# First norm applied on leaving PSUM, its transposes inside the first two projection slots, masks by quarters

## The chip, the cores and the metric

The kernel runs on one core of a Trainium2 chip. The metric is its device time in microseconds (us). The engines are TensorE (PE, its weight loads PEld), VectorE (DVE), ScalarE (ACT), GpSimd (POOL) and SyncE (SP), which only issues transfers here. Each works through its own list of instructions in order and waits on semaphores.

## What is computed

A decoder trunk of two layers on 1024 tokens of width 1024, all in float32. The first layer's mixer is what the change touches:

```
def rmsnorm(x, g):
    xf = x.astype(jnp.float32)
    y = xf * lax.rsqrt(jnp.mean(xf * xf, axis=-1, keepdims=True) + EPS)
    return (y * g.astype(jnp.float32)).astype(x.dtype)
...
    h = rmsnorm(x, norm_mix[layer])
    if layer % 2 == 0:
        x = x + even_mixer(h, positions, ...)
    ...
    h = rmsnorm(x, norm_mlp[layer])
    x = x + sq_relu_mlp(h, mlp_w_up[layer], mlp_w_down[layer])
```

`even_mixer` projects h and splits the columns into 4 retention heads and 8 heads of dilated attention, whose queries and keys are normed and rotated. A query sees the keys at distances 0, 1, .. 128, at multiples of 4 up to 512 and at multiples of 16 up to 2048; a key seen by two or three patterns counts twice or three times. So the score of a distance gets a summand that depends on the distance alone: nothing, minus log 2 or log 3, or a large number that takes the key out (the scores are kept negated). Then follow the output projection, an MLP, and the second layer with windowed attention and an MLP.

## The kernel before

Tokens stand in T = 8 tiles of 128 partitions, X[:, i, :]. Every product is done in three passes over split operands: a matrix is kept as a rounded part (hi) and the rest (lo), and hi*hi + hi*lo + lo*hi is summed in PSUM. Weights come in by SyncE into `raw` in pieces of two blocks of 128 rows (128 x 768 for a projection). ScalarE writes W_hi (`split_hi`, L620), GpSimd writes W_lo (`split_lo`, L1209), and SyncE may load the next but one piece when W_lo of a piece is done (`w_ready`).

The start (phase DR) works like this. GpSimd fills a table of distances `di` (L1313) and small constants. VectorE's `masks` makes `nlm`, the summand by distance, for all 1024 distances in 14 instructions (L867 to L886). ScalarE makes 16 exponentials for the retention decay (L806 to L809). Then for each of the eight token tiles ScalarE squares and sums (`square`, L626), GpSimd takes the root (`norm_rstd`, L1214, L1216), VectorE multiplies by the token's factor and the gain (`normed`, L943), TensorE transposes eight blocks (L360) into `sc` or `tp` in turn, ScalarE copies the rounded part to hT_hi (L630) and VectorE writes hT_lo (`lo_T`, L933). Only then are the four pieces of the first projection split, and VectorE computes the angles (L891 to L918).

After that `dr_slots` runs 66 slots. Slot s projects one token tile (24 matmuls, 128x384 each, L350 to L352): slots 0 to 7 those of two heads of dilated attention, 8 to 15 those of one retention head, and so on for four groups. In slot t, ScalarE evacuates the product of slot t-1 into G (`evac_G`, L637) and squares it (L652); VectorE sums (L1006), GpSimd multiplies by the gains (L1225) and takes the roots (L1239, L1241), VectorE norms and rotates (`prep`, L1015 to L1027), TensorE transposes (`heads_T`, L441) and ScalarE copies these to qT and kT. Two units of attention go along, each in steps: `scores` (L400), `maxima` (L1044), `probs` (L672), `trans` (L422), `probs_T` (L664), `values` (L434), `outputs` (L1064, L1066). A new `values` waits until `outputs` of the unit before has read o_ps. In slots 2 to 5 of each eight a piece of the next weights is split as well.

What sets the order is the order in which each engine's function writes its instructions: there is no scheduler. Slot by slot and half by half (j = 0, 1), each engine's `dr_slots` lists its steps.

## Time and profile before

| | us |
|---|---|
| median of 3 runs | 2614.97 |
| lowest and highest | 2613.98, 2615.36 |
| the profiled execution | 2612.44 |
| its span | 2610.7 |
| TensorE busy in it | 2486.2 (95%) |
| VectorE, ScalarE, GpSimd busy | 1075.7, 739.6, 806.7 |

The page says how busy each engine is in 40 slices of 65 us; the chain of waits follows the last instruction back to the start; the timeline lists instructions with their start, duration and what ended the idle time before them. Times are from the start of the span. A matmul's duration reaches beyond the start of the next, so the distance of two starts tells the pace.

### The profile page before, as it was taken

The numbers are of one execution on the slowest core, as the hardware profiler recorded it, in microseconds if no ns is written. First come the engines' busy times: TensorE is split into PE (matmuls) and PEld (weight loads), VectorE is DVE, ScalarE is ACT, GpSimd is POOL, SyncE is SP. The second block draws the span as 40 slices with busy tenths as digits, with TensorE's granted clock in tenths as the row PEclk, the third lists the DMA queues.
The fourth block names the chain that finished last, engine by engine and source line by source line (L and its number), as shares of the span: only waits on it lengthen the run. The fifth ranks groups of instructions, "written<-read, shape, count | busy, mean of one in ns | idle before, by whom it ended". The sixth has DMA issues, their size and how long they took to land.

```text
span 2610.7 us, 34016 instructions
## 1 busy us (share of the span) xinstructions
PE 2486.2 (95%) x12520; PEld 2080.3 (80%) x12520; DVE 1075.7 (41%) x2591; ACT 739.6 (28%) x1487; POOL 806.7 (31%) x770
## 2 busy tenths in 40 slices
PE   5999999998989999999999799999989999999998
PEld 4787878787968888888887688879978888888886
DVE  7464645454323232323233566662322323232323
ACT  4424343331221212121221355552312121212220
POOL 4223132310333333333332233331133333333331
PEclk9999999998999999999999899998999999999999
DMA  3000000002211111111111200003011111111111
GB/s 115 25 25 25 25 25 25 25 19 80 69 33 49 48 48 48 48 48 48 48 48 43 89 26 25 25 25 103 31 49 49 48 48 48 48 48 48 48 48 65
DMA packets 108200, 120.20 MB, mean 46 GB/s; under 512 B 26048, under 2 KB 94144, under 8 KB 108096
## 3 DMA queue, kind: packets, MB, share of 16 engines
q1 hardware_dynamic: 100720, 103.70, 12.8%
q10 hardware_dynamic: 7376, 15.12, 1.7%
q8 instruction: 64, 1.05, 0.2%
q14 instruction: 40, 0.33, 0.0%
HBM read 110.41 MB, written 8.39 MB: 46 GB/s over the span
## 4 chain that ended last, share of the span: by engine, by line
PE 84%; DVE 8%; POOL 3%; ACT 2%; issue 2%; DMA 0%; POOLq 0%; SPq 0%; ACTq 0%; DVEq 0%
PE gp L350 11%; PE gp L352 10%; PE gp L351 10%; PE sc L350 5%; PE sc L352 4%; PE sc L351 4%; PE tp L351 4%; PE tp L352 4%; PE tp L350 4%; PE o_ps L434 4%; PE sc L400 3%; PE tp L422 2%; PE o_ps L350 2%; PE qt L350 2%; PE qt L351 2%; PE o_ps L352 2%
## 5 line engine op out<-in xcount | busy, mean ns | idle before, releaser
L1209 POOL TENSOR_TENSOR W_lo<-raw,W_hi 128x1024 fp32r<-128x1024 f32 (+2 forms) x200 | 433.7, 2183 | 704.1 <-ACT W_hi L620 704.0
L350 PE MATMUL gp<-W_hi,hT_hi 128*128 128x384 f32 (+1 forms) x1152 | 421.9, 366 | 14.8 <-POOL W_lo L1209 6.7
L352 PE MATMUL gp<-W_hi,hT_lo 128*128 128x384 f32 (+1 forms) x1152 | 384.3, 334 | 0.0
L351 PE MATMUL gp<-W_lo,hT_hi 128*128 128x384 f32 (+1 forms) x1152 | 383.9, 333 | 0.0
L620 ACT ACTIVATE W_hi<-raw 128x1024 fp32r<-128x1024 f32 (+2 forms) x200 | 186.4, 964 | 646.7 <-PE qt L352 559.0
L1148 DVE TENSOR_TENSOR r<-r 128x512 f32<-128x512 f32 x128 | 92.2, 720 | 626.8 <-ACT r L773 626.8
L1295 POOL TENSOR_TENSOR a_lo<-r,a_hi 128x512 fp32r<-128x512 f32 x128 | 166.0, 1298 | 447.5 <-ACT a_hi L775 447.5
L1155 DVE TENSOR_TENSOR X<-tp,X 128x512 f32<-128x512 f32 x256 | 176.8, 692 | 173.8 <-PE tp L352 171.7
L350 PEld LDWEIGHTS gp<-W_hi,hT_hi 128*128 128x128 f32 x1152 | 221.2, 192 | 26.9 <-issue 11.2
L351 PEld LDWEIGHTS gp<-W_lo,hT_hi 128*128 128x128 f32 x1152 | 221.6, 192 | 0.0
L352 PEld LDWEIGHTS gp<-W_hi,hT_lo 128*128 128x128 f32 x1152 | 219.9, 191 | 0.0
L350 PE MATMUL gp<-hT_hi,W_hi 128*128 128x512 f32 x512 | 201.5, 393 | 16.0 <-POOL W_lo L1209 16.0
L350 PE MATMUL tp<-W_hi,a_hi 128*128 128x512 f32 x512 | 204.1, 399 | 11.7 <-POOL W_lo L1209 11.7
L350 PE MATMUL sc<-hT_hi,W_hi 128*128 128x512 f32 x512 | 200.9, 392 | 5.3 <-DVE hT_lo L933 5.3
L351 PE MATMUL tp<-W_lo,a_hi 128*128 128x512 f32 x512 | 204.1, 399 | 0.0
L352 PE MATMUL tp<-W_hi,a_lo 128*128 128x512 f32 x512 | 203.9, 398 | 0.0
L352 PE MATMUL gp<-hT_hi,W_lo 128*128 128x512 f32 x512 | 200.4, 391 | 0.0
L352 PE MATMUL sc<-hT_hi,W_lo 128*128 128x512 f32 x512 | 200.4, 391 | 0.0
L351 PE MATMUL sc<-hT_lo,W_hi 128*128 128x512 f32 x512 | 200.2, 391 | 0.0
L351 PE MATMUL gp<-hT_lo,W_hi 128*128 128x512 f32 x512 | 200.1, 391 | 0.0
L434 PEld LDWEIGHTS o_ps<-V,pT 128*128 128x128 f32 x1056 | 138.5, 196 | 15.8 <-issue 8.7
L434 PE MATMUL o_ps<-V,pT 128*128 128x64 f32 x1056 | 136.8, 274 | 11.1 <-DVE X L1066 7.0
(187 smaller groups left out, 4083.8 us busy)
## 6 DMA issues: line engine op xcount, KB each, us to landing
raw<-in_mlp_w_up SPq DMA_DIRECT2D x64, 512.0 KB, 3.8
raw<-in_mlp_w_down SPq DMA_DIRECT2D x64, 512.0 KB, 3.2
raw<-in_hyb_w_in SPq DMA_DIRECT2D x80, 128.0 KB, 2.5
X<-in_x SPq DMA_DIRECT2D x8, 512.0 KB, 12.0
X<-in_x ACTq DMA_DIRECT2D x8, 512.0 KB, 3.2
raw<-in_swa_w_qkv SPq DMA_DIRECT2D x16, 256.0 KB, 2.7
x_spill<-X ACTq DMA_DIRECT2D x8, 512.0 KB, 2.6
X<-x_spill ACTq DMA_DIRECT2D x8, 512.0 KB, 3.3
```

The source lines that it names most:

```text
L350: mm(o, a[0], b[0], start=first, stop=False)
L351: mm(o, a[0], b[1], start=False, stop=False)
L352: return mm(o, a[1], b[0], start=False, stop=last)
L400: last = mm(sc[:, c:e], qT[r, a % 2, 0:P], kT[r, c:e], start=True, stop=True)
L422: last = nc.tensor.transpose(tp[:, to:to + P], Pm[:, j, c:c + P], ident[:, :])
L434: last = mm(o_ps[:, e * HD:(e + 1) * HD], pT[:, j, to:to + P], V[:, c, v0:v0 + HD], start=(m == 0 or bl[m - 1][3] != e), stop=(m == len(bl ...
L620: A(W_hi[:, slot, n * p:n * (p + 1)], raw[:, p % 2, 0:n], ACT.Copy).then_inc(w_hi, 1)
L1148: E.tensor_tensor(r2[:, ft, :], r2[:, ft, :], r2[:, ft, :], ALU.mult).then_inc(a_sq, 1)
L1155: E.tensor_tensor(x, d_out[(2 * i + nh) % D_BANKS], x, ALU.add).then_inc(d_evac, 1)
L1209: E.tensor_tensor(W_lo[:, slot, c], raw[:, p % 2, 0:n], W_hi[:, slot, c].bitcast(f32), ALU.subtract).then_inc(w_ready, 1)
L1295: E.tensor_tensor(a_lo[par][:, ft, r], r2[:, ft, :], a_hi[par][:, ft, r].bitcast(f32), ALU.subtract).then_inc(a_ready, 1)
```

## The change

The norm of the first layer's mixer is taken apart. The gain is multiplied in ahead of the transposes (`first_gain`, into a new buffer xn0), while the token's factor, a number per row of the product, is applied by ScalarE when it evacuates the projection (`evac_G`, now with a scale from `nscale`). Tiles 0 and 2 get their gain from VectorE, 1 and 3 to 7 from GpSimd. The transposes of tile 0 come ahead of the first slot, those of the others at places inside slots 0 and 1 (`FIRST_T`). The squares and roots of tiles 2 to 7 move to the ends of slots 1 to 6. The pieces of the first weights are loaded and split between the first token tiles. `masks` makes only the last 256 of 1024 columns of nlm, which the first units of attention read, and `far_masks` makes the other three quarters in slot 3, ahead of `outputs`. The exponentials (`powers`) move with the load of the retention gains from the start to the end of slot 7, and what VectorE does with them (`decays`) to the start of slot 8. W_hi and W_lo get other addresses, so that xn0, the gain g0 and the angles lie in halves of them that aren't used yet. In the diff, "..." marks what is left out.

```diff
-            sp.dma_start(gA[:, :], bcast(norm_mix[0], D)).then_inc(g_full, 16)
-            for i in range(1, T):
+            sp.dma_start(g0[:, :], bcast(norm_mix[0], D)).then_inc(g_full, 16)
+            load_D(0, P_DR, (0, 1))
+            for i in range(1, 4):
                 sp.dma_start(X[:, i, :], xt[:, i, :]).then_inc(x_full[i], 16)
-            load_D(0, P_DR)
+            load_D(0, P_DR, (2, 3))
+            for i in range(4, T):
+                sp.dma_start(X[:, i, :], xt[:, i, :]).then_inc(x_full[i], 16)
             load_R(0, P_DR + 4)
             for g in range(1, NG):
...
+            def first_T(s, q):
+
+                for i in range(T):
+                    if FIRST_T[i] == (s, q):
+                        norm_T(0, i, 0, 0)
+
+            FIRST_T = [(0, 0), (0, 2), (0, 4), (1, 1), (1, 2), (1, 3), (1, 4), (1, 4)]
...
+                        if s < 2 and j == 0:
+                            first_T(s, 0)
                         next(steps)
                         next(steps)
+                        if s < 2:
+                            first_T(s, 2 * j + 1)
...
-                A(G[:, (t - 1) % RING, :], gp[:, (t - 1) % 2, 0:W], ACT.Copy).then_inc(gemm_evac, 1)
+                i = (t - 1) % T
+                act.wait_ge(rstd_ready, i + 1)
+                A(G[:, (t - 1) % RING, :], gp[:, (t - 1) % 2, 0:W], ACT.Identity,
+                  scale=nscale[:, i:i + 1]).then_inc(gemm_evac, 1)
...
+            def powers():
+
+                act.wait_ge(ss_ready, T)
+                act.dma_start(gnB, bc(gn_gain[0].rearrange("h d -> (h d)"), RH * RV)).then_inc(const_in, 16)
+                for h in range(RH):
+                    A(decay[:, h, :], dq[:, 0:P], ACT.Exp, scale=LG[h])
+                    A(xi[:, h:h + 1], dq[:, P:P + 1], ACT.Exp, scale=LG[h])
+                    A(zeta[:, h:h + 1], dq[:, P + 1:P + 2], ACT.Exp, scale=LG[h])
+                    last = A(cdec[:, h:h + 1], dq[:, P + 2:P + 3], ACT.Exp, scale=LG[h])
+                step.did(last)
...
+                            if s == 1:
+                                for i in ((3, 4), (5, 6, 7))[j]:
+                                    copy_T(i, 0, 0)
                             if j == 1 and 0 <= t - 1 < T:
                                 heads_T_copy("D", t, a0)
+                        if j == 1 and 1 <= s < T - 1:
+                            square(0, s + 1)
+                        if j == 1 and s == T - 1:
+                            powers()
...
-            for i in range(T + 1):
-                if i < T:
-                    act.wait_ge(x_full[i], 16)
-                    square(0, i)
-                if i >= 1:
-                    copy_T(i - 1, 0, 0)
-            for p in range(4):
-                split_hi(p, 0, W, 16 * KQ * (p // 2 + 1))
+            for p in range(2):
+                split_hi(p, 0, W, 16 * KQ)
+                copy_T(p, 0, 0)
+                act.wait_ge(x_full[p], 16)
+                square(0, p)
+            for p in (2, 3):
+                split_hi(p, 0, W, 2 * 16 * KQ)
             act.wait_ge(dve_step, SETUP_SIN)
...
+            def mask_of(o, counts):
+                step.wait()
+                step.did(E.tensor_scalar(o, t2[:, :], 0.0, BIG, ALU.is_equal, ALU.mult))
...
+            def far_masks():
+
+                step.did(E.tensor_tensor(t2[:, :], m4[:, :], m16[:, :], ALU.add))
+                mask_of(nlm[:, 2 * MW:3 * MW], (2.0,))
+                step.wait()
+                step.did(E.scalar_tensor_tensor(t2[:, :], df[:, :], 512.0 - 2 * MW, m4[:, :], ALU.is_le, ALU.mult))
+                step.wait()
+                step.did(E.tensor_tensor(t2[:, :], t2[:, :], m16[:, :], ALU.add))
+                mask_of(nlm[:, MW:2 * MW], (2.0,))
+                step.did(E.tensor_scalar(nlm[:, 0:MW], m16[:, :], 0.0, BIG, ALU.is_equal, ALU.mult))
+                step.wait()
...
+            def decays():
+                dve.wait_ge(act_step, 2)
                 dve.wait_ge(const_in, 16 * 5)
...
+            def first_gain(i):
+                dve.wait_ge(g_full, 16)
+                dve.wait_ge(x_full[i], 16)
+                if i >= 2:
+                    dve.wait_ge(nt_done, i - 1)
+                E.tensor_tensor(xn0[:, i % 2, :], X[:, i, :], g0[:, :], ALU.mult).then_inc(xn_ready, 1)
...
+                    if s == T:
+                        decays()
                     for j in range(2):
+                        if s == 3 and j == 1:
+                            far_masks()
...
             masks()
-            for i in range(T + 1):
-                if i < T:
-                    normed(0, i, 0)
-                if i >= 1:
-                    lo_T(i - 1, 0, 0)
+            first_gain(0)
+            lo_T(0, 0, 0)
             angles()
+            lo_T(1, 0, 0)
+            first_gain(2)
+            lo_T(2, 0, 0)
...
+                        if s == 1:
+                            for i in (5, 6, 7):
+                                first_gain(i)
...
-                norm_rstd(0, i)
-            for p in range(4):
-                split_lo(P_DR, p, 0, 2 * W)
-            pool.wait_ge(const_in, 16 * 5)
+            split_lo(P_DR, 0, 0, 2 * W)
+            split_lo(P_DR, 1, 0, 2 * W)
+            first_gain(1)
+            norm_rstd(0, 0)
+            norm_rstd(0, 1)
+            split_lo(P_DR, 2, 0, 2 * W)
+            split_lo(P_DR, 3, 0, 2 * W)
+            first_gain(3)
+            first_gain(4)
+            pool.wait_ge(const_in, 16 * 4)
...
```

On TensorE, the end of the first transposes and the start of the first product, before (xnA is the normed tile, sc and tp the halves of PSUM that take transposes):

```order
L360 MATMUL sc<-ident,xnA 128x128 [waits ht_ready,xn_ready]
L360 MATMUL sc<-ident,xnA 128x128 x7
L360 MATMUL tp<-ident,xnA 128x128 [waits ht_ready,xn_ready]
L360 MATMUL tp<-ident,xnA 128x128 x7
L350 MATMUL gp<-W_hi,hT_hi 128x384 [waits w_ready,ht_ready,gemm_evac]
L351 MATMUL gp<-W_lo,hT_hi 128x384
L352 MATMUL gp<-W_hi,hT_lo 128x384
```

And after, in the middle of slot 0 (xn_75 is xn0):

```order
L365 MATMUL gp<-W_hi,hT_hi 128x384
L366 MATMUL gp<-W_lo,hT_hi 128x384
L367 MATMUL gp<-W_hi,hT_lo 128x384
L375 MATMUL tp<-ident,xn_75 128x128 [waits xn_ready]
L375 MATMUL tp<-ident,xn_75 128x128 x7
L365 MATMUL gp<-W_hi,hT_hi 128x384 [waits w_ready]
L366 MATMUL gp<-W_lo,hT_hi 128x384
L367 MATMUL gp<-W_hi,hT_lo 128x384
```

The transposes of tile 1 now stand between the fourth and fifth block of slot 0's product, and the product waits there for its weights.

On ScalarE, from the first evacuation (G<-gp) to the second and the first exponential of the attention, before:

```order
L637 ACTIVATE G<-gp 128x384 [waits gemm_done]
L652 ACTIVATE sq<-G 128x256 [waits gemm_evac]
L686 ACTIVATE qT<-qt 128x128 [waits qt_done]
L688 ACTIVATE kT<-qt 128x128
L637 ACTIVATE G<-gp 128x384 [waits gemm_done]
L652 ACTIVATE sq<-G 128x256 [waits h_ss,gemm_evac]
L672 ACT_TABLE_LOAD
L672 ACTIVATE Pm,st<-Pm,st 128x128 [waits sm_ready]
```

And after:

```order
L672 ACTIVATE G<-gp,st 128x384 [waits rstd_ready,gemm_done]
L688 ACTIVATE sq<-G 128x256 [waits gemm_evac]
L663 ACTIVATE hT_hi<-tp 128x8x128 [waits nt_done]
L663 ACTIVATE hT_hi<-sc 128x8x128 [waits nt_done]
L663 ACTIVATE hT_hi<-tp 128x8x128 [waits nt_done]
L663 ACTIVATE hT_hi<-sc 128x8x128 [waits nt_done]
L663 ACTIVATE hT_hi<-tp 128x8x128 [waits nt_done]
L722 ACTIVATE qT<-qt 128x128 [waits qt_done]
L724 ACTIVATE kT<-qt 128x128
L659 ACTIVATE c,st<-X 128x1024 [waits ss_ready]
L672 ACTIVATE G<-gp,st 128x384 [waits rstd_ready,gemm_done]
L688 ACTIVATE sq<-G 128x256 [waits h_ss,gemm_evac]
```

Five copies of transposed tiles and tile 2's square now stand between the two evacuations.

On VectorE in slot 3, from the end of `prep` to `outputs` of unit 0 and the next maxima, before:

```order
L1027 TENSOR_TENSOR QK<-ropeA,ropeB 128x4x16 [waits dve_step]
L1064 RECIPROCAL st<-st 128x1 [waits pv_done]
L1066 TENSOR_SCALAR X<-o_ps,st 128x64 [waits dve_step]
L1044 ISA Pm,st<-sc,nlm 128x256 [waits tp_done,s_done]
L1044 ISA st 128x1
```

And after (m_87 and m_88 are the marks of multiples of 4 and 16, t_84 and t_85 scratch):

```order
L1094 TENSOR_TENSOR QK<-ropeA,ropeB 128x4x16 [waits dve_step]
L938 TENSOR_TENSOR t_85<-m_87,m_88 128x256
L929 TENSOR_SCALAR nlm<-t_85 128x256 [waits dve_step]
L932 TENSOR_SCALAR t_84<-t_85 128x256 [waits dve_step]
L934 TENSOR_TENSOR nlm<-nlm,t_84 128x256 [waits dve_step]
L941 SCALAR_TENSOR_TENSOR t_85<-df,m_87 128x256 [waits dve_step]
L943 TENSOR_TENSOR t_85<-t_85,m_88 128x256 [waits dve_step]
L929 TENSOR_SCALAR nlm<-t_85 128x256 [waits dve_step]
L932 TENSOR_SCALAR t_84<-t_85 128x256 [waits dve_step]
L934 TENSOR_TENSOR nlm<-nlm,t_84 128x256 [waits dve_step]
L945 TENSOR_SCALAR nlm<-m_88 128x256
L1131 RECIPROCAL st<-st 128x1 [waits pv_done,dve_step]
```

The ten instructions of `far_masks` have come between the rotated heads and the division that frees o_ps.

## Rows read from the trace of the kernel before

**Rows 1.** Page, busy tenths of TensorE in 40 equal slices of the span.
```profile
PE   5999999998989999999999799999989999999998
```

**Rows 2.** Timeline 0 to 17 us: start us, us, engine, line, operation, out<-in, count, [idle<-releaser].
```profile
1.92 0.71 DVE L867 TENSOR_SCALAR di<-di 128x1024 int32<-128x1024 int32 x1 [1.92 <-POOL di L1313]
...
13.83 1.23 DVE L886 TENSOR_TENSOR nlm<-nlm,t 128x1024 f32<-128x1024 f32 x1
...
14.97 2.48 DVE L943 SCALAR_TENSOR_TENSOR xnA<-X,st,gA 128x1024 f32<-128x1024 f32 x2
```

**Rows 3.** Timeline, the loop over token tiles, 22 to 42 us.
```profile
22.72 1.97 PE L360 MATMUL sc<-ident,xnA 128*128 128x128 f32 x8 [2.68 <-DVE xnA L943]
...
24.73 1.03 ACT L630 ACTIVATE hT_hi<-sc 128x1024 fp32r<-128x1024 f32 x1 [2.34 <-PE sc L360]
...
25.65 1.05 ACT L626 ACTIVATE junkA<-X 128x1024 f32<-128x1024 f32 x1
...
40.82 1.23 DVE L933 TENSOR_TENSOR hT_lo<-tp,hT_hi 128x1024 fp32r<-128x1024 f32 x1 [1.10 <-ACT hT_hi L630]
```

**Rows 4.** Timeline, first product, and transposes of tile 0's heads.
```profile
43.55 0.66 PE L350 MATMUL gp<-W_hi,hT_hi 128*128 128x384 f32 x1 [3.83 <-POOL W_lo L1209]
...
58.70 0.42 PE L441 MATMUL qt<-ident,QK 128*128 128x128 f32 x2
```

**Rows 5.** Timeline, end of slot 2 and slot 3.
```profile
65.43 0.44 PE L441 MATMUL qt<-ident,QK 128*128 128x128 f32 x2 [0.82 <-DVE QK L1027]
...
69.47 0.42 DVE L1015 TENSOR_TENSOR QK<-QK,st 128x256 f32<-128x256 f32 x1 [1.25 <-POOL st L1241]
...
69.67 1.91 POOL L1209 TENSOR_TENSOR W_lo<-raw,W_hi 128x768 fp32r<-128x768 f32 x1 [0.31 <-ACT W_hi L620]
...
69.93 1.73 DVE L1022 TENSOR_TENSOR ropeA<-QK,cosD 128x64 f32<-128x64 f32 x1
...
72.67 0.41 PE L434 MATMUL o_ps<-V,pT 128*128 128x64 f32 x2 [1.00 <-DVE X L1066]
```

**Rows 6.** DMA view of issues at 1.25, 1.71 and 3.52 us: KB each, us to landing.
```profile
gA<-in_norm_mix SPq DMA_DIRECT2D x1, 512.0 KB, 6.1
...
X<-in_x SPq DMA_DIRECT2D x1, 512.0 KB, 8.0
...
c<-in_ret_gn_gain ACTq DMA_DIRECT2D x1, 256.0 KB, 12.7
```

**Rows 7.** Groups by form, GpSimd: count | busy us, mean ns | idle before.
```profile
L1209 POOL TENSOR_TENSOR W_lo<-raw,W_hi 128x1024 fp32r<-128x1024 f32 x128 | 305.2, 2405 | 543.5 <-ACT W_hi L620 543.5
```

**Rows 8.** Chain of waits, 134 to 136 us: start us, us, what.
```profile
134.10 1.02 PE tp L422 x8
135.12 0.17 PE gp L350
```

**Rows 9.** Timeline, slot 4.
```profile
78.28 1.72 DVE L1027 TENSOR_TENSOR QK<-ropeA,ropeB 128x64 f32<-128x64 f32 x1
...
80.55 0.63 PE L434 MATMUL o_ps<-V,pT 128*128 128x64 f32 x4
```

**Rows 10.** Timeline, slot 5.
```profile
86.37 0.23 DVE L1027 TENSOR_TENSOR QK<-ropeA,ropeB 128x64 f32<-128x64 f32 x1
...
86.63 1.82 POOL L1209 TENSOR_TENSOR W_lo<-raw,W_hi 128x768 fp32r<-128x768 f32 x1 [1.29 <-ACT W_hi L620]
```

**Rows 11.** Stretch 52 to 53 us: busy PE, PEld, DVE, ACT, POOL; granted clock, DMA share, GB/s.
```profile
52.00:53.00 1.00, 1.00 (x3) 1.00 (x4) 0.93 (x4) 0.00 (x1) 0.00 (x0) 0.50 0.70 185
```

**Rows 12.** Timeline, TensorE, 52 to 53 us.
```profile
52.43 0.52 PE L351 MATMUL gp<-W_lo,hT_hi 128*128 128x384 f32 x1
52.75 0.52 PE L352 MATMUL gp<-W_hi,hT_lo 128*128 128x384 f32 x1
```

**Rows 13.** Timeline, ScalarE, first and last of the sixteen exponentials.
```profile
6.80 0.31 ACT L806 ACTIVATE c<-dq 128x128 f32<-128x128 f32 x1
...
8.65 0.19 ACT L809 ACTIVATE st<-dq 128x1 f32<-128x1 f32 x1
```

More of the change, by code:

```diff
@@ L252, in rows, with runs @@
                 return w.rearrange("(d q) n -> q d n", q=P)[:, n * p:n * (p + 1), :]
-            def runs(w, parts, first):
-                for p in range(4):
+            def runs(w, parts, first, pieces=range(4)):
+                for p in pieces:
                     free(first, p)
@@ L589, in _ @@
             pe.wait_ge(pool_step, SETUP_ID)
-            for i in range(T):
-                norm_T(0, i, 0, 0)
             dr_slots()
```

109 lines of the change are left out of this document (66 added, 43 removed).

## The prediction

> **What bounds the kernel now.** I read the page's slices first: TensorE is nearly full everywhere but in the first one [rows 1]. So the change can only save in the first 59 us. There the timeline comes next. The masks keep VectorE from 1.92 to 15.06 us [rows 2], and the first gain, transposes and copies stand behind them. Then comes a loop over token tiles that ends at 42.05 (40.82 + 1.23) [rows 3]. The first product starts at 43.55, and the transposes of tile 0's heads (L441), my mark for the end of slot 1, at 58.70 [rows 4]. From slot 2 on the same mark stands at 65.43, and in slots 2 to 5 TensorE doesn't run free: slot 3's `values` starts at 72.67 after 1.00 us of waiting for VectorE [rows 5]. Those slots were the part to look at twice, since the change puts work there.
>
> **What it saves ahead of slot 2.** I lay the new order out with durations of rows.
> Masks: 14 instructions took 13.1 us at 1024 columns. A two-tensor one takes 0.42 at 256 [rows 5] against 1.23 [rows 2], a third, so 15 take about 5.5 us and end near 7. The gain vector lands at 1.25 + 6.1 = 7.35 [rows 6], so the first gain ends at 8.6, and tile 0's transposes (1.97) at 10.6. Copy 1.03 and subtraction 1.23 [rows 3] put the first product at 13.0, 30 us earlier than 43.55.
> It doesn't last, because each step then waits on another engine. The first weight piece takes the place of X's second tile, which landed at 1.71 + 8.0 = 9.7 [rows 6]; with 384 KB for 512 I take 9.2. Its low part (GpSimd, 1.82 undisturbed [rows 10]) is there at 12.0. ScalarE then has tile 0's copy and square (1.05 and the reading of its sum, 1.15 in all) before it rounds piece 1 (ends 13.7), whose low part ends at 15.9. GpSimd's own first gain, tile 1, is a two-tensor pass of 1024 columns: 2.41 in the row of that size [rows 7], against 2.48 for two of them on VectorE [rows 2]. It ends at 18.7, tile 1's transposes at 20.6, copy at 21.7, square at 22.9, rounding of piece 2 at 23.7, low parts of pieces 2 and 3 at 25.7 and 28.7 (VectorE's gain of tile 2 goes between them). Slot 0's last product ends at 30.7, tile 2's transposes at 32.7.
> Slot 1, with products at TensorE's faster spacing and transposes at 1.0 for eight [rows 8]: tile 3 done 34.8, tile 4 37.0. The gain of tile 5 stands on GpSimd behind the head gains and rstd of tile 0, which need slot 0's evacuation (34.3): 37.3 to 39.7; tile 6's ends at 42.5, tile 7's at 45.1. VectorE's small rope instructions for tile 0 stand ahead of tile 5's subtraction and are held by GpSimd's passes, as in slot 3, where one took 1.73 that began 0.26 after a W_lo [rows 5], for 0.23 when free [rows 10]. So that subtraction ends at 47.0, tile 7 at 48.1, and the mark comes at 48.1 against 58.70: **10.6 us earlier**. Ends: 50.3 if every product of slots 0 and 1 runs at the slower spacing, 45.2 if all run at the faster one (without the holds another us or two less).
> The Trainium skill (GPSIMD Engine Reference, section 1, Specifications) says that GpSimd and VectorE share their SBUF interfaces, with contention for VectorE instructions of two SBUF inputs or in a two-port mode. The subtraction from PSUM has one such input; by that rule it isn't held, and I don't hold it.
>
> **Slot 2.** ScalarE now squares tile 2 (1.15) before it evacuates, and copies tile 7 after its late transposes; scores wait for all eight tiles (50.4). Evacuation ends 2.8 us after the mark; squares, sums, GpSimd's rstd (behind the new norm rstd), and a rope held once by a W_lo put the next mark at 57.1 against 65.43: **8.3 us earlier**.
>
> **What slots 3 to 5 give back.** (a) In slot 3 the square puts the evacuation 1.15 us later; the norm's rstd on GpSimd adds 0.3 to the rstd of the heads. The rope ends some 1.45 later. (b) Then `far_masks`, ten instructions of 256 columns, stands ahead of `outputs` of unit 0, for which TensorE waits already [rows 5]. Five with two tensors at 0.46 and five with one at about 0.3 make 3.8 us (ends: 10/14 of a third of 13.1, 3.1; ten at 0.46, 4.6). Nothing covers it. Slot 3 loses 1.45 + 3.8 = **5.3**.
> (c) In slot 4 the last rope instruction is held already (1.72 [rows 9]) and TensorE starts `values` at 80.55, right after VectorE's output. With the chain 1.5 later and W_lo 1.1 later the hold stays, so this slot loses up to 1.9. I take **1.9**, end 0.
> (d) In slot 5 the rope has just ended when W_lo starts (86.37 + 0.23 against 86.63 [rows 10]). Later by 1.6, with W_lo later by 1.1 to 1.2, it falls under it, and the output comes about 1.4 after TensorE wants it. It hangs on 0.1 us: I take half, **0.7**, ends 0 and 1.4.
> (e) TensorE idles over 6 us in slot 3. Before, after the waits of the first slot, the granted clock was 0.50 at 52 to 53 [rows 11], the 1.2 GHz level: matmuls 0.32 apart [rows 12] instead of 0.17 to 0.18 [rows 8]. I take six products' worth, 6 x 0.145 = **0.8**, ends 0 and 2. The Trainium skill (TensorE: Matmul & The Clock Gate, Part 1) says that an idle array falls back to half rate. Its own sample spacings, 107 and 56 ns, make it a factor of 1.9, and (e) would be 0.8 by it too; what it adds is that the fall is to be expected.
> (f) Slots 6 and 7: the chain is 1.2 later, but no W_lo stands there and TensorE is full; nothing. Slot 8: ScalarE runs `powers` (16 short instructions and a DMA issue, 2.6 us: they took from 6.80 to 8.84 [rows 13], and an issue costs some 0.6) ahead of an evacuation, and VectorE's `decays` waits for them and for 256 KB of gains. VectorE comes 2.6 us later; the scores behind it are needed some 3 us later, so nothing again, if the gains land in 3 us. They took 12.7 before [rows 6], but with all of X in the queues.
> The copy with a scale in place of a plain copy I count at nothing: same size, same engine, and the built order has three table loads as before. From group 1 on nothing differs.
>
> **Sum.** -8.3 + 5.3 + 1.9 + 0.7 + 0.8 = +0.4. The profiled execution has a span of 2610.7 and a time of 2612.44, 2.5 under the median of 2614.97, so I add the difference to the median: **2615.4**, rounded 2615.5. The 30 us at the start are given back twice, first to the chain through four engines, then to the work moved into slots that VectorE sets.
>
> **The rivals.**
> 1. *The gain stays.* The GpSimd passes slip in beside the rope, so the holds of slots 1, 4 and 5 don't fall, and the clock stays up: mark at 45.2, less (c), (d), (e): 2.9 + 1.9 + 0.7 + 0.8 = 6.3 under the forecast, 2609. For it: the slot 5 hold hangs on 0.1 us, and the front was laid out with the slower clock. Against: GpSimd got ahead of the rope in slots 3 and 4 of before [rows 5, 9]. Chance 0.20.
> 2. *The clock stays down* (slower). TensorE works in short pieces from 8 to 48 us and stops in slot 3. If it runs at 1.2 GHz in slots 1, 2 and 4 as in the first products, that is 2.2 more in slot 1 (50.3 against 48.1), about 1 in slot 2, where 24 x 0.145 = 3.5 is mostly under the chain, and 3.5 in slot 4, bare: 6.7, 2622. It makes the kernel slower by over 0.2% from some 33 bare matmuls at half speed (4.8 / 0.145). For it: [rows 11, 12]. Against: with no wait, before was back at full spacing 3 us later. Chance 0.15.
> 3. *The gain vector of the retention norm lands late* in slot 8 (slower). At 12.7 us of landing, VectorE would stand till 125 with its queue, scores' maxima first, against 115: some 7 us over its slack, 2622. Against: DMA is almost idle then. Chance 0.04.
> The forecast with its bounds has 0.58; 0.03 is left for what I don't see, on both sides.
>
> **How the numbers follow.** 0.2% is 5.2 us, about what a measurement tells from no change. The forecast's own range: best 8.3 + 2.9 saved, 4.6 lost, 2608.5; worst 6.1 saved, 6.1 + 1.9 + 1.4 + 2 lost, 2620; most of it lies within 0.2%. With rivals 1 and 2 at their edges I give 2608 to 2622. Faster: rival 1 mostly, 0.20. Slower: rivals 2 and 3 and a little of the forecast's edge, 0.19. Within 0.2%: 0.61.
>
> **What would show it.** First product near 13, mark of slot 1 near 48, of slot 2 near 57; TensorE idle 5 to 7 us in slot 3 ahead of `values`, released by VectorE's output, with ten mask instructions before it; a slot 3 of 13 us against 8.07; waits of 1 to 2 us for the same output in slots 4 and 5; from slot 6 on both profiles one constant apart, near zero. I am wrong if the mark of slot 1 comes before 45 or after 51, if the masks fall into idle time of both engines, or if the distance still changes after slot 8.

## The result

| | before | after |
|---|---|---|
| median, us | 2613.23 | 2622.23 |
| lowest and highest | 2610.44, 2616.20 | 2615.29, 2625.37 |
| executions | 13 | 13 |
| the profiled execution: span, time | 2610.7, 2612.44 | 2623.5, 2625.37 |

The ratio is 1.0027, with a 95% interval of 1.0019 to 1.0036: the change makes the kernel 9.0 us slower, where I forecast no difference. The median lies 0.2 us above the upper end of my range (2608 to 2622), and the profiled execution 3.4 above it. That 2622 stood in the prediction at all is luck: it was the total of a rival whose loss sat in other slots.

The page of after, TensorE's busy tenths and granted clock (the same two kinds of line of before below it; the first is [rows 1]):

```profile
PE   5999999998989999999999799999989999999998
PEclk8999999998999999999999899998989999999999
```
```profile
PEclk9999999998999999999999899998999999999999
```

At 65 us a digit the two kernels look the same but for the clock, a tenth lower in the first slice and in one later one. So the transposes of the heads were the next thing to read, my mark for the end of a slot. In after, TensorE's timeline over the first 125 us (start, duration, line, operation, [idle before <- releaser]):

```profile
14.70 0.66 PE L365 MATMUL gp<-W_hi,hT_hi 128*128 128x384 f32 x1 [4.63 <-DVE hT_lo L1000]
25.97 0.69 PE L365 MATMUL gp<-W_hi,hT_hi 128*128 128x384 f32 x1 [4.91 <-POOL W_lo L1285]
38.86 1.09 PE L375 MATMUL tp<-ident,xn 128*128 128x128 f32 x8 [2.10 <-POOL xn L1302]
45.34 1.94 PE L375 MATMUL tp<-ident,xn 128*128 128x128 f32 x8 [2.79 <-DVE hT_lo L1000]
47.07 0.64 PE L458 MATMUL qt<-ident,QK 128*128 128x128 f32 x2
56.24 0.38 PE L458 MATMUL qt<-ident,QK 128*128 128x128 f32 x2
68.59 0.66 PE L451 MATMUL o_ps<-V,pT 128*128 128x64 f32 x2 [4.89 <-DVE X L1133]
70.12 0.63 PE L458 MATMUL qt<-ident,QK 128*128 128x128 f32 x2
79.83 0.38 PE L458 MATMUL qt<-ident,QK 128*128 128x128 f32 x2
111.09 0.38 PE L458 MATMUL qt<-ident,QK 128*128 128x128 f32 x2
116.58 1.52 PE L451 MATMUL o_ps<-V,pT 128*128 128x64 f32 x12 [1.02 <-DVE X L1133]
124.58 0.38 PE L458 MATMUL qt<-ident,QK 128*128 128x128 f32 x2
```

Against the marks of before the distance runs:

| mark of slot | 1 | 2 | 3 | 4 | 5 | 6 | 7 | 8 | end |
|---|---|---|---|---|---|---|---|---|---|
| before | 58.70 | 65.43 | 73.50 | 81.59 | 90.54 | 100.59 | 111.73 | 123.94 | 2610.7 |
| after | 47.07 | 56.24 | 70.12 | 79.83 | 89.66 | 99.95 | 111.09 | 124.58 | 2623.5 |
| difference | -11.6 | -9.2 | -3.4 | -1.8 | -0.9 | -0.6 | -0.6 | +0.6 | +12.8 |

The front did much as the sum said: 11.6 us won by the mark of slot 1, 2.4 of it given back in slot 2 and 8.3 in slots 3 to 5. Then slot 8 lost 1.3, and 12 us more went in a stretch in which the two kernels issue the same work in the same order. That stretch had no term in my sum.

### The profile page after: what moved, and what is told of

Read it like the earlier page. It is cut to its first block, busy times and chain, and to the rows that moved or that the text cites. A ratio compares the mean times of both kernels' runs of the same rounds, so it can differ in the third digit from the quotient of the medians.

```text
span 2623.5 us, 34066 instructions
## 1 busy us (share of the span) xinstructions
PE 2497.7 (95%) x12520; PEld 2085.9 (80%) x12520; DVE 1071.5 (41%) x2596; ACT 742.9 (28%) x1487; POOL 817.6 (31%) x776
## 3 DMA queue, kind: packets, MB, share of 16 engines
q1 hardware_dynamic: 100720, 103.70, 12.8%
## 4 chain that ended last, share of the span: by engine, by line
PE 83%; DVE 8%; POOL 4%; issue 2%; ACT 2%; DMA 1%; POOLq 0%; SPq 0%; ACTq 0%; DVEq 0%
PE gp L365 11%; PE gp L366 10%; PE gp L367 10%; PE sc L365 5%; PE sc L367 5%; PE sc L366 5%; PE tp L365 4%; PE tp L366 4%; PE tp L367 4%; PE o_ps L451 4%; PE sc L417 2%; PE tp L439 2%; PE o_ps L365 2%; PE o_ps L366 2%; PE o_ps L367 2%; PE qt L367 2%
## 5 line engine op out<-in xcount | busy, mean ns | idle before, releaser
L365 PE MATMUL gp<-W_hi,hT_hi 128*128 128x384 f32 (+1 forms) x1152 | 428.2, 372 | 18.0 <-DVE hT_lo L1000 7.0
```

The costliest lines, as they stand in the source:

```text
L365: mm(o, a[0], b[0], start=first, stop=False)
```

## Experiments

All times below are medians. Before was run beside each group of kernels: 2613.88 for experiments 1 to 4, 2613.83 for 5 to 7, 2613.43 for 8 to 10 and 2614.77 for 11 and 12. For each kernel two numbers matter: where slot 8's mark stands against before, and how much the median moved beyond that, "behind slot 8".

**1. Only shift the program.** Before, with two fills on GpSimd ahead of the table of distances, which hold up the masks and so all that follows.

```diff
+            for n in range(2):
+                E.memset(hT_lo[:, n, :].bitcast(f32), 0.0)
             step.did(E.iota(di[:, :], ...
```

> The kernel before, with two fills of 1024 columns on GpSimd ahead of everything else. Nothing else differs, so the whole program starts about 2 us later. Theory (the clock's phases): what the changed kernel lost behind slot 8, 12 us in its profiled run with the same instructions, comes from when TensorE's stops fall; then this kernel too shows stretches at 1.2 GHz of other lengths than the kernel before, at the starts of the attention groups and at the stage changes, and its time moves by something else than the delay, by up to some 8 us either way. Rival (something in the change that lasts): the time rises by the 2 us and the distance of the two profiles stays flat from the first product to the end.

Measured: 2616.5 (ratio 1.0009, 0.9999 to 1.0019). Slot 8's mark is 1.08 later, where I had expected some 2, and the same instructions then cost 1.5 more. The interval takes in 1, so the median alone doesn't show the 1.5; the profiles of the two kernels do show steps of 1.1 to 1.5 us at single stops (at 198 and 480 us), and some back.

**2. Only the addresses.** Before, with W_hi and W_lo allocated behind the small constants, as in after. They move from byte 82048 of each partition to 137728; raw, X and nlm move down.

```diff
-        W_hi = sb("W_hi", [P, 2, KD * W], f32r)
-        W_lo = sb("W_lo", [P, 2, KD * W], f32r)
...
+        W_hi = at("W_hi", [P, 2, KD * W], f32r)
+        W_lo = at("W_lo", [P, 2, KD * W], f32r)
+        A0 = off[0]
         RING = 4
```

> The kernel before, with W_hi and W_lo at the addresses that the change gives them and nothing else. Theory (clock phases): within 2 us of the kernel before, and the profiles level. Rival (lasting cost of the new addresses): 5 to 9 us slower, gathered steadily over the projections and the MLPs.

Measured: 2618.44 (1.0016, 1.0006 to 1.0026). It is 4.6 us slower. The mark of slot 8 is 1.4 later, and 3.2 more go behind it. Where shifting alone left long stretches without a stop of TensorE at a constant distance from before (4.44 at 830 us and 4.45 at 1420), here the distance grows: 3.40 at 830, 4.14 at 1400. After does the same, 5.22 to 5.96. This was the first sign that one cause lies in the addresses.

**3. The far masks out of the way.** After, with `far_masks` in three parts behind the work of slots 3, 5 and 6.

```diff
-                        if s == 3 and j == 1:
-                            far_masks()
...
                             if j == 1 and 0 <= r < T:
                                 ret_state(g, r, g * T + r)
+                        if j == 1 and s in (3, 5, 6):
+                            far_masks({3: 2, 5: 1, 6: 0}[s])
```

> The changed kernel with its far masks in three parts, each behind the attention work of its half slot, in slots 3, 5 and 6, where VectorE has idle time, and not ahead of the division in slot 3. By the prediction's term (b), slot 3 takes 9.3 to 9.8 us and not 13.9, TensorE waits about 1 us there and not 4.9, and the mark of slot 7's end comes 4 to 5 us earlier. If the masks had been hidden, nothing moves. The whole time follows only if the clock lets it: 3 to 6 us less in the mean, by the clock theory with several us of scatter.

Measured: 2615.5 (1.0009, 1.0000 to 1.0019). Slot 3 takes 9.56 us for 13.88, so 4.3 of its loss go with the masks, where I had 3.8. The masks themselves take 3.8 in after; the rest is in part the lower clock behind the stop (0.50 from 68.3 to 71.7 in after, none there in this kernel). Slot 8's mark stands 5.8 ahead of before, and the end 1.6 behind: 7.4 lost where nothing differs.

**4. The exponentials a slot earlier as well.** Experiment 3, and:

```diff
-                        if j == 1 and s == T - 1:
+                        if j == 1 and s == T - 2:
                             powers()
```

> As the kernel with the far masks behind, and the exponentials with their load of the retention gains one slot earlier, at the end of slot 6. VectorE at the start of slot 8 then waits for no transfer, and the 1.3 us that slot 8 lost go: slot 8 takes 12.2 us again. With both, the mark of slot 8 stands some 5 us ahead of the kernel before; the whole should be faster than it by 3 to 5 us if the clock costs the same, and not at all if the stops later in the program cost more.

Measured: 2619.17 (1.0023, 1.0013 to 1.0033). Slot 8 falls to 12.24 us, the 12.21 of before, so its loss is this block's; but slot 7 takes 14.7 (96.07 to 110.77) for the 11.1 of experiment 3. The block only moves, and slot 7 is 3.6 longer, with the clock at 0.50 from 103.4 to 106.8 in it. Slot 8's mark is 0.9 ahead of before, where I had expected some 5. Behind slot 8: 6.2.

**5. Only the evacuation with a scale.** Before, with the evacuation of after and a column of ones.

```diff
-                A(G[:, (t - 1) % RING, :], gp[:, (t - 1) % 2, 0:W], ACT.Copy).then_inc(gemm_evac, 1)
+                act.wait_ge(rstd_ready, (t - 1) % T + 1)
+                A(G[:, (t - 1) % RING, :], gp[:, (t - 1) % 2, 0:W], ACT.Identity,
+                  scale=nscale[:, (t - 1) % T:(t - 1) % T + 1]).then_inc(gemm_evac, 1)
```

> The kernel before with only the evacuation of the projection in the form of the change: wait for the token's root, then a copy with a scale per row (a column of ones). Its result is the same. The profile of after loses 1.3 us in small amounts between 190 and 600 us of before and again 0.3 to 0.9 between 1515 and 1760, which the kernel before with the change's addresses hardly does. If this evacuation is the cause, the distance to before grows here by 1 to 1.3 us between 190 and 600, with the marks of slots 1 to 8 within 0.3 of before, and the median is some 2615. If it is not, the distance is a constant but for steps of about 1.2 us at TensorE's stops (198, 340, 480, 760, 1440 to 1515, 1776, 1920), and the median is 2612 to 2617 by the steps alone.

Measured: 2612.02 (0.9997, 0.9988 to 1.0007). The mark is 0.2 early, behind it 1.6 are won. The scaled evacuation is not the cause of the 9 us. It isn't free either: it takes 0.58 us for the 0.49 of the plain copy, and TensorE waits 0.2 to 0.3 us longer for VectorE at three places (212, 220 and 359 us). The distance to before grows by 0.5 between 210 and 330 us and by 0.2 between 352 and 450, where experiment 1 stays within 0.03.

**6. After, with the old addresses.**

```diff
+        wh0 = nc.sbuf_base
+        W_hi = sb("W_hi", [P, 2, KD * W], f32r)
+        wl0 = nc.sbuf_base
+        W_lo = sb("W_lo", [P, 2, KD * W], f32r)
         raw = sb("raw", [P, 2, 1024])
...
-        wh0 = off[0]
-        W_hi = at("W_hi", [P, 2, KD * W], f32r)
-        wl0 = off[0]
-        W_lo = at("W_lo", [P, 2, KD * W], f32r)
```

> The kernel after, with W_hi and W_lo (and with them raw, X, nlm and the small constants behind them) at the addresses of before; xn0, g0 and the angles still lie in the unused halves. If the addresses cost the slow drift, the MLP between 830 and 1400 us runs at a constant distance from before (after: +0.74, the kernel before with the change's addresses: +0.74, without them: +0.00), the drift after 1960 goes too, and the median falls by 1.2 to 3 us to 2619 to 2621. If the drift belongs to something else, the distance grows by 0.74 again and the median stays at 2622. Slot 8's mark stays at 124.6 by both. Steps of about 1.2 us at TensorE's stops are expected by the theory of the clock whatever the addresses, 2 to 7 us in all, so the median alone doesn't decide; the MLP does.

Measured: 2616.18 (1.0009, 1.0000 to 1.0018), 6.0 under after, though slot 8's mark came 1.3 us later than in after. The distance between 830 and 1400 us stays at 1.33. After stood 9.0 above before, this kernel 2.3: 6.7 of the 9.0 us go with the addresses alone (either ratio is known to some 2.3 us). What is lost behind slot 8 falls from 8.4 to 0.4.

The mark came later for a reason of its own. In slot 4 of this kernel TensorE never waits, yet the slot takes 11.32 us for 9.71. Its windows (length, busy us and count of each engine, granted clock, DMA share, GB/s):

```profile
65.00:70.00 5.00, 1.73 (x6) 1.67 (x7) 3.67 (x13) 0.60 (x2) 0.00 (x0) 0.72 0.19 52
70.00:75.00 5.00, 5.00 (x15) 3.48 (x15) 0.98 (x3) 2.80 (x8) 2.72 (x6) 0.50 0.00 0
75.00:80.00 5.00, 5.00 (x23) 4.21 (x22) 1.96 (x9) 1.46 (x4) 1.98 (x2) 0.76 0.10 28
```

After the stop for the masks the clock was at 1.2 GHz through the whole of 70 to 75, with 15 matmuls for 23 in the same window of after (clock 0.83). That is my second rival's mechanism, in an execution whose slot 3 ended at 69.80, much like that of after (70.12).

**7. Old addresses, far masks behind, gains loaded earlier.** Experiments 3 and 6 together, and the load of the retention gains issued one slot before `powers`.

```diff
+                        if j == 1 and s == T - 2:
+                            act.wait_ge(ss_ready, T)
+                            act.dma_start(gnB, ...).then_inc(const_in, 16)
                         if j == 1 and s == T - 1:
                             powers()
```

> The kernel after with the addresses of before, the far masks in three parts behind the work of slots 3, 5 and 6, and the load of the retention gains issued one slot before the exponentials. Slot 8 took 13.49 us with the load right ahead of the exponentials and 12.2 in before; so the mark of slot 8 should stand at 116.9, 7.1 us before that of before (118.14 in the kernel with the masks moved). If the rest of the program lost only what addresses cost, the end would be 7 us under before, 2607. By the theory of the clock's steps every kernel whose program is shifted loses 2 to 5 us more than before at the same seven stops: 2609 to 2612. If the whole gain is lost again, as in the kernel with the masks moved (-5.8 at slot 8, +1.6 in the median), it is 2614 to 2615, and there must be a cause for it that doesn't depend on addresses.

Measured: 2612.14 (0.9996, 0.9987 to 1.0005). Slot 8's mark is only 4.4 ahead of before, not 7.1: slot 1's came 1.8 later than in experiment 3, and slot 8 took 12.8. In slot 8 TensorE's wait for VectorE's output is 0.31 for 1.01, but the slot is only 0.7 shorter, not 1.3. Behind slot 8: 2.7, against 7.4 in experiment 3 with the new addresses.

**8. Squares off the chain.** Experiment 7 with the squares of tiles 2 to 7 at the end of a slot's first half, where ScalarE waits 2 to 3 us, and their roots behind W_lo on GpSimd. The load of the retention gains is issued half a slot later than in experiment 7, behind the last square.

```diff
-                        if j == 1 and 1 <= s < T - 1:
-                            square(0, s + 1)
-                        if j == 1 and s == T - 2:
+                        if j == 0 and 2 <= s < T:
+                            square(0, s)
+                        if j == 0 and s == T - 1:
...
-                    if 1 <= s < T - 1:
-                        norm_rstd(0, s + 1)
+                    if 2 <= s < T:
+                        norm_rstd(0, s)
```

> The kernel c_all with the squares of tiles 2 to 7 at the end of the first half of slots 2 to 7 (ScalarE waits 2 to 3 us there) in place of right ahead of an evacuation, and their roots behind W_lo on GpSimd. The prediction put 1.45 us of slot 3's loss down to the square and root ahead of the heads' chain. If that is right, slots 3, 4 and 5 take 8.1, 8.1 and 8.95 us as in before (c_all: 9.56, 9.46, 9.84), slot 8's mark moves from 119.5 to some 115.5, and the median from 2612.1 to 2608. If it was the rope held by W_lo that made them long, little changes: 0.5 us a slot, 118 and 2611. If the gain is lost behind slot 8 whatever stands ahead, the median stays at 2612.

Measured: 2605.83 (0.9975, 0.9964 to 0.9985). Slots 3, 4 and 5 take 7.97, 8.30 and 8.95 us for 9.56, 9.46 and 9.84, and in before 8.07, 8.09 and 8.95. So the square and the root cost 1.6, 1.2 and 0.9 a slot, with what they change in the holds: in slot 5 of experiment 7 and of after W_lo holds a rope instruction (1.85 and 1.86 us), here and in before none. In experiment 7 TensorE waits 0.36 in slot 5 ahead of that hold and 0.06 behind it, so the hold is the smaller part.

**9. Gains on VectorE.** Experiment 8, and VectorE makes the gains of tiles 3 to 7.

```diff
             first_gain(2)
+            first_gain(3)
+            first_gain(4)
             lo_T(2, 0, 0)
...
                                 for i in ((3, 4), (5, 6, 7))[j]:
+                                    if i < 6:
+                                        first_gain(i + 2)
                                     lo_T(i, 0, 0)
...
```

> As d_off_chain, and VectorE makes the gains of tiles 3 to 7 (1.23 us each, with nothing on GpSimd beside them) in place of GpSimd (2.4 us each, with VectorE's passes held at 1.9 to 2.4 us beside them). In c_all the transposes of tiles 5 and 6 wait 2.11 and 0.46 for GpSimd's gains and those of tile 7 2.79 behind VectorE's held rope. I expect slot 1's mark at 42 to 44 (c_all: 47.6), the scores' release at 46 to 47 (50.3), slot 8's mark 3 to 4 us before that of d_off_chain, some 112, and the median 2604 to 2605. The rival: the gain is lost in slot 2 because VectorE's copies of tiles 5 to 7 stand ahead of the heads' sums; then slot 8's mark is at 114 to 115 and the median 2607.

Measured: 2602.61 (0.9959, 0.9945 to 0.9972). Slot 1's mark stands at 43.64 and slot 8's at 111.90, 12.0 ahead of before, as expected; behind it only 1.2 are lost.

**10. The same with the new addresses.** The diff is that of experiment 6, the other way round.

> d_all with W_hi and W_lo (and raw, X, nlm and the small constants) at the addresses of after, nothing else. It tests the addresses a third time: before to its copy with the new addresses cost 4.6 us in the median, of which 1.4 came ahead of slot 8; after against after with the old addresses 6.0. By the theory of the addresses this one is 3 us slower than d_all or more (3.0 is the sum of what the steady products lose in the traces), with the MLP from 830 to 1400 us 0.74 us longer. By the theory that only the clock's steps differ from kernel to kernel, it is within 2.5 us on either side, and the MLP has the same length.

Measured: 2607.24 (0.9978, 0.9968 to 0.9987), 4.6 above d_all, with slot 8's mark 0.2 later. The three pairs give, behind slot 8, 3.2 (before), 7.9 (after) and 4.4 (d_all) for the addresses.

What the addresses do can be read off groups of equal matmuls in the first MLP, from 850 to 1400 us, where the granted clock is 1.00 in all of these kernels. TensorE's groups (out<-in, tile, shape, count | busy, mean ns of one | idle), three each of before and of experiment 2:

```profile
L352 PE MATMUL sc<-hT_hi,W_lo 128*128 128x512 f32 x208 | 81.0, 389 | 0.0
L350 PE MATMUL gp<-hT_hi,W_hi 128*128 128x512 f32 x206 | 80.4, 390 | 0.0
L351 PE MATMUL tp<-W_lo,a_hi 128*128 128x512 f32 x193 | 76.2, 395 | 0.0
```
```profile
L352 PE MATMUL gp<-hT_hi,W_lo 128*128 128x512 f32 x208 | 82.2, 395 | 0.0
L350 PE MATMUL sc<-hT_hi,W_hi 128*128 128x512 f32 x203 | 80.2, 395 | 0.0
L351 PE MATMUL tp<-W_lo,a_hi 128*128 128x512 f32 x192 | 74.8, 389 | 0.0
```

Products of the weights with hT (up) and with the hidden values a (down) have changed places. The distance of their starts shows the same 6 ns: up 227 and down 232.5 in before, 233 and 227 with the new addresses (means of some 1200 each). The projections, 128x384, go from 175.0 to 176.0 in the first phase and from 173.6 to 175.9 in the output projection.

**11. The two slots of the weights apart.** d_all with slot 0 of W_hi and W_lo at the old place, behind hT, and slot 1 at the new one, ahead of a.

```diff
+        hi0 = sb("hi0", [P, KD * W], f32r)
+        lo0_ = sb("lo0_", [P, KD * W], f32r)
...
+        hi1 = at("hi1", [P, KD * W], f32r)
+        lo1 = at("lo1", [P, KD * W], f32r)
+        W_hi, W_lo = [hi0, hi1], [lo0_, lo1]
```

> d_all with the two weight slots apart: slot 0 of W_hi and W_lo at the old place (bytes 82048 to 106624 of a partition, right behind hT), slot 1 at the new one (162304 to 186880, right ahead of the MLP's hidden values a at 186880 and up). In the traces so far matmuls that take weights and hT (up) start 227 ns apart with weights at the old place and 233 at the new; those that take weights and a (down) 232.5 and 227. Both at full clock. Theory of sides: two operands on one side of a line between 131200 and 137728 cost 227, on two sides 233. Then the first MLP (up in slot 1, down in slot 0) has 233 and 232.5, and the second (up in slot 0, down in slot 1) has 227 and 227. Rival, the pace belongs to W as a whole: both MLPs look alike, one kind fast and one slow. In the median the first MLP loses 7 us to before and the second gains 7, the projections in slot 1 lose some: 2603 to 2607.

Measured: 2603.43 (0.9957, 0.9944 to 0.9971). TensorE's groups in the first MLP (850 to 1400), and then in the second (1990 to 2540):

```profile
L369 PE MATMUL sc<-hT_lo,hi 128*128 128x512 f32 x208 | 82.1, 395 | 0.0
...
L368 PE MATMUL tp<-hi,a_hi 128*128 128x512 f32 x195 | 76.9, 395 | 0.0
```
```profile
L369 PE MATMUL gp<-hT_lo,hi 128*128 128x512 f32 x208 | 80.9, 389 | 0.0
...
L368 PE MATMUL tp<-hi,a_hi 128*128 128x512 f32 x200 | 77.8, 389 | 0.0
```

In the first MLP, which takes its up weights from slot 1 and its down weights from slot 0, both are slow. In the second, the other way round, both are fast. That is what the theory of sides forecast: the pace depends on where the weights lie against the other operand, not on W as a whole.

**12. W up by 8192 bytes.** d_all, and:

```diff
+        raw = sb("raw", [P, 2, 1024])
         W_hi = sb("W_hi", [P, 2, KD * W], f32r)
         W_lo = sb("W_lo", [P, 2, KD * W], f32r)
-        raw = sb("raw", [P, 2, 1024])
```

> d_all with raw (8 KB) ahead of W_hi, so that W moves up by 8192 bytes: slot 1 of W_lo at 127104 to 139392, all else of W below 127104. If the line lies near 131072 bytes, as the theory of sides has it, then in the second MLP the up products (slot 0) keep 227 ns and of the down products the sixth that reads the second half of slot 1's low part is fast: 231.5 in the mean; in the first MLP the up products (slot 1) have a sixth at 233 (blocks 4 to 7 of the low part): 228, the down ones 232.5. If distance between operands or an alignment of another size counts, the paces change in another way or not at all (a shift of 8192 bytes keeps every alignment up to 8 KB). The median within 2 us of d_all, 2602.6; 1 us more if the projections in slot 1 lose.

Measured: 2601.32 (0.9952, 0.9938 to 0.9965), the fastest of all, though not to be told from d_all. The paces are those of d_all in all four products (227.0, 232.4, 227.1, 232.4), with the weights of slot 1 reaching byte 135296. So a line at 131072 is wrong. Nor do the projections show one further up. The last block of W_lo's slot 1 in the first phase lies at bytes 137856 to 139392 here, above the 137728 where W begins in after, and the matmuls that read it (32 of 128x384) start 173.7 ns before the next, as in d_all (173.7) and before (173.8); with the new addresses it is 175.8 and 176.6 (experiments 10 and 2). So a line across all addresses isn't shown, and by the projections is unlikely. Which property of the two addresses decides it, their distance for one, stays open.

## Where the 9 us are

The addresses have a steady part that is shown, and may have one at the stops. The steady part: in the stretches without a stop of TensorE (130 to 190, 210 to 330, 352 to 450, 500 to 600, 625 to 700, 830 to 1400, 1515 to 1760, 1790 to 1890 and 1960 to 2560) the distance grows by 3.6 us from before to its copy with the new addresses and by 2.8 from after with the old ones to after, which has one wait of 1.45 for W_lo at 1821 in it that after doesn't have. Without the steps at which TensorE waits it is 3.2 and 3.7, and 3.9 for the pair of d_all. I take 3.5.

The rest comes at the stops, and it goes in the main with the clock. At 198 us group 1 begins with a stop of 3.1 us in both kernels. Windows of before and then of after (the clock is the third number from the end):

```profile
198.00:200.00 2.00, 2.00 (x9) 1.56 (x7) 0.42 (x1) 1.25 (x4) 0.73 (x1) 0.62 0.00 0
200.00:202.00 2.00, 2.00 (x8) 1.78 (x7) 0.72 (x3) 1.20 (x3) 1.21 (x2) 0.53 0.00 0
202.00:204.00 2.00, 2.00 (x12) 1.63 (x11) 1.98 (x3) 0.04 (x1) 1.82 (x1) 1.00 0.00 0
```
```profile
198.00:200.00 2.00, 1.56 (x6) 1.56 (x7) 0.35 (x3) 0.84 (x3) 0.00 (x0) 0.50 0.00 0
200.00:202.00 2.00, 2.00 (x7) 1.34 (x6) 0.47 (x2) 0.50 (x2) 1.36 (x3) 0.50 0.00 0
202.00:204.00 2.00, 2.00 (x7) 2.00 (x7) 1.49 (x7) 1.23 (x3) 1.00 (x2) 0.50 0.00 0
204.00:206.00 2.00, 2.00 (x10) 1.62 (x9) 1.50 (x1) 0.00 (x0) 1.42 (x1) 0.79 0.00 0
```

And of the kernel before with the scaled evacuation:

```profile
198.00:200.00 2.00, 2.00 (x12) 1.63 (x11) 0.53 (x2) 1.30 (x4) 0.73 (x1) 1.00 0.00 0
200.00:202.00 2.00, 2.00 (x12) 1.67 (x10) 0.61 (x3) 1.24 (x3) 1.76 (x3) 1.00 0.00 0
```

One and the same stop costs nothing, 1.7 us or 3.4 us of lost clock (the sum over the windows of one minus the clock, times the length). The time lost isn't the same number: from before the stop to behind it (190 to 205 us) after falls back by 1.4 us against before, and experiment 5 gains 0.3 though it saves 1.7 of clock. Kernels share an outcome without sharing an edit: after and experiment 7, whose programs stand 5 us apart there and whose addresses differ, both lost 3.4. Experiments 5, 8 and 9 show one run of steps, 0.35 down here and 1.1 to 1.2 up at 345, though the programs of 5 and 9 stand 12 us apart. The sum over all stops behind slot 8, beside what the profiled execution lost there against before (difference of the spans less that of slot 8's marks). Experiment 11, with one slot of weights at each place, is left out:

| kernel | lost clock | more than before | lost in all |
|---|---|---|---|
| before | 47.8 | 0 | 0 |
| 5, scaled evacuation | 46.1 | -1.7 | -0.7 |
| 9, d_all | 47.8 | 0 | 1.2 |
| 8, squares off the chain | 47.8 | 0 | 1.4 |
| 6, after with old addresses | 51.2 | 3.4 | 1.4 |
| 12, W up by 8192 bytes | 49.5 | 1.7 | 1.5 |
| 1, shifted | 52.9 | 5.1 | 3.4 |
| 7, old addresses | 54.6 | 6.8 | 7.0 |
| 2, new addresses | 47.8 | 0 | 2.4 |
| 3, new addresses | 49.5 | 1.7 | 7.3 |
| 10, new addresses | 51.2 | 3.4 | 9.5 |
| 4, new addresses | 51.2 | 3.4 | 9.6 |
| after, new addresses | 58.0 | 10.2 | 12.1 |

With 3.5 added for the new addresses the third column gives the fourth to within 2.7 us. That is no proof that clock alone makes the steps, because some of them come at full clock. Before and then after, around 1503 and 1510 us:

```profile
1502.78 1.86 POOL L1209 TENSOR_TENSOR W_lo<-raw,W_hi 128x768 fp32r<-128x768 f32 x1 [1.51 <-ACT W_hi L620]
1502.79 0.15 DVE L1071 TENSOR_TENSOR st<-st 128x2 f32<-128x2 f32 x1
```
```profile
1509.22 1.82 POOL L1285 TENSOR_TENSOR W_lo<-raw,W_hi 128x768 fp32r<-128x768 f32 x1 [1.50 <-ACT W_hi L652]
1509.24 1.82 DVE L1138 TENSOR_TENSOR st<-st 128x2 f32<-128x2 f32 x1
1511.73 0.63 PE L451 MATMUL o_ps<-V,pT 128*128 128x64 f32 x4 [1.22 <-DVE X L1142]
```

In before a VectorE instruction on two columns slips in beside W_lo, in after it is held for W_lo's whole 1.82 us, and the distance grows by 1.4. At 344 a hold in after costs 1.0; at 483 one in before costs 1.2 that after doesn't lose. Behind slot 8 TensorE idles 87.9 us in before and 90.2 in after, and from 87.4 to 93.5 in the others. Clock and holds aren't separated here.

One profiled execution of each kernel is a sample: kernels with eight or more executions spread by 4 to 10 us. What I can't show is why after loses more at the stops in its median than its copy with the old addresses, beyond the steady part: 7.9 less 3.5 leaves 4.4, while the pair of before leaves -0.3 and that of d_all 0.9. That stays open.

So of the 9.0 us in the median: 0.6 stand at slot 8's mark, some 3.5 are steady and come from the addresses, and the remaining 5, found by subtraction, come at and around the stops, in half-speed stretches and waits for VectorE.

## The prediction, point by point

**The front was right.** First product: 13.0 forecast, 14.70 measured. Slot 1's mark: 48.1, 47.07, with TensorE waiting for GpSimd's gains and then for a subtraction behind VectorE's held rope, as laid out. In after, VectorE's timeline:

```profile
39.12 2.37 DVE L1089 TENSOR_TENSOR ropeA<-QK,cosD 128x64 f32<-128x64 f32 x1
41.41 0.18 DVE L1090 SCALAR_TENSOR_TENSOR ropeB<-QK,sinD 128x32 f32<-128x32 f32 x1
41.51 0.18 DVE L1091 TENSOR_TENSOR ropeB<-QK,sinD 128x32 f32<-128x32 f32 x1
41.72 2.34 DVE L1094 TENSOR_TENSOR QK<-ropeA,ropeB 128x64 f32<-128x64 f32 x1
43.98 1.21 DVE L1000 TENSOR_TENSOR hT_lo<-tp,hT_hi 128x1024 fp32r<-128x1024 f32 x1
```

Beside them GpSimd's gains run from 39.03 to 41.40 and from 41.63 to 43.98, and two rope instructions of 64 elements take 2.4 us each. The subtraction at 36.79, beside a gain from 36.45 to 38.80, took 1.22, its usual time. By the Trainium skill (GPSIMD Engine Reference, section 1, Specifications), VectorE contends with GpSimd only with two SBUF inputs or in a two-port mode; on the rope, with two SBUF inputs, and on the subtraction, with one, the trace agrees.

**Slots 3 to 5: right in sum, wrong in a cause.** I had 5.3, 1.9 and 0.7 given back, 7.9 in all; the three slots took 33.42 us for 25.11, 8.3 more. The masks with the clock behind them are 4.3 of it by experiment 3 (3.8 forecast for the masks, and 64.16 to 67.93 in the trace), and the square and root in slot 3 are 1.6 by experiment 8 (1.45 forecast). What I put down to the held rope in slots 4 and 5 was mainly the same square and root again, 1.2 and 0.9 by experiment 8; I had charged them to slot 3 only. Slot 5's rope did fall under W_lo, as step (d) had it (1.86 us from 85.52, beside a W_lo from 85.48), but behind it TensorE waited only 0.04. TensorE's wait in slot 3 was 4.89, not 5 to 7. First and last of the ten mask instructions, and the output behind them:

```profile
64.16 0.42 DVE L938 TENSOR_TENSOR t<-m,m 128x256 f32<-128x256 f32 x1
...
67.64 0.29 DVE L945 TENSOR_SCALAR nlm<-m 128x256 f32<-128x256 f32 x1
67.96 0.16 DVE L1131 RECIPROCAL st<-st 128x1 f32<-128x1 f32 x1
68.16 0.28 DVE L1133 TENSOR_SCALAR X<-o_ps,st 128x64 f32<-128x64 f32 x1
```

**Step (f), slot 8: 0 forecast, 1.3 measured.** The load of the gains did land in 3.1 us, as the step asked, but VectorE stands in its own queue for that, and behind it is the output that frees o_ps, not only the scores I had looked at. ScalarE's DMA issue, then VectorE, in after:

```profile
111.52 0.33 ACTq L729 DMA_DIRECT2D c<-in_ret_gn_gain  x1
```
```profile
114.62 1.13 DVE L985 TENSOR_TENSOR c<-c,tri 128x512 f32<-128x512 f32 x1 [5.20 <-DMA c<-in_ret_gn_gain]
115.67 0.25 DVE L987 TENSOR_SCALAR st<-st 128x4 f32<-128x4 f32 x1
115.95 0.16 DVE L1131 RECIPROCAL st<-st 128x1 f32<-128x1 f32 x1
116.15 0.28 DVE L1133 TENSOR_SCALAR X<-o_ps,st 128x64 f32<-128x64 f32 x1
```

TensorE waits 1.02 for that output, as the fence in the section on the result shows. With the load a slot earlier it waits 0.31 (experiment 7).

**"From group 1 on nothing differs" is the step that failed**, and with it "both profiles one constant apart". The instructions are the same, their addresses aren't, and I passed over a line of the diff that I had described myself. It costs 6.7 us of 9.0 by experiment 6, and 4.6 in either of the other two pairs; the steady 3.5 of it is shown product by product, the rest only in the medians. The prediction did say what would show it, the distance still changing after slot 8.

The copy with a scale, put at nothing for its equal size, is a smaller miss: 0.58 us for 0.49, and some 0.7 us between 210 and 450 (experiment 5).

**The second rival** had the mechanism that much of the rest went into, in the wrong place. I priced the half clock in slots 1, 2 and 4 at 6.7 us. In after it cost little there, since the slots wait for VectorE anyway (slot 4 took 9.71); it came at the stops of later stages, where I had no price. Step (e), 0.8, priced one stop, while the stops behind slot 8 hold 47.8 us of lost clock in before and 58.0 in after. That this rival's total, 2622, is the measured median is chance. The Trainium skill (TensorE: Matmul & The Clock Gate, Part 1) says that an idle array falls back to half rate; the trace agrees, but not always: with the scaled evacuation it stayed at full rate through the same stop at 198 us.

**The first rival** fell: the clock and the holds were as forecast, and the gain went.

## What to carry to other kernels

A move of a buffer is an edit with a price: time one group of equal matmuls before and after it, at full clock, ahead of all arithmetic on the schedule. A gain in the ramp of a kernel is worth what is left of it at the first slot that TensorE fills, so list for each later slot what now stands ahead of the instruction that frees a PSUM buffer; here that, with the old addresses, turned 9 us slower into 11 us faster (experiment 9). Below half a per cent, shifted programs draw different half-speed stretches and other VectorE holds at each stop, and a difference of 5 us in one profile says little without a second kernel that differs in nothing but the shift.

## What the runs showed of the hardware

The pace of back-to-back float32 matmuls of 128x512 at full clock is 227 or 232.5 to 233 ns, and where the two operands lie in SBUF decides it: weights at 82048 to 135296 with hT at 16512 to 82048 are fast and with a at 186880 and up slow; weights at 137728 to 186880 the other way round. By which rule isn't known. The Trainium skill (TensorE: Matmul & The Clock Gate, Part 2) says that TensorE reads its two operands through two independent ports, so that loading the next weights takes no bandwidth from the running matmul. By that alone no place should be slower than another; the runs show 2.5%.

The cost of a stop of TensorE of 3.1 us isn't one number. The clock's part of it was 0, 1.7 or 3.4 us at the same stop, in kernels with the same instructions around it but for the form of an evacuation and the addresses, and the time lost there isn't the same number.

An elementwise instruction of GpSimd with two SBUF inputs holds a VectorE instruction with two SBUF inputs for its whole length, however short that one is: 1.82 us for 0.15 at 1509 us in after. In before the VectorE instruction started 0.01 us after GpSimd's and wasn't held, in after 0.02 and was.
